# The per-token rows of an mLSTM head, copied to all partitions by DMA inside SBUF instead of by products, and the next head's weights moved right behind the scores

## The reference

```
m_t = max(max_s d, b + m_old)          d = b_t - b_s + i_s   (s <= t)
w   = exp(d - m_t)                      s = (q k) * w
num = sum_s s v + inter part            den = sum_s s + inter part
h   = num / max(|den|, exp(-m_t))       then RMSNorm of h over the head's 256 channels
```

## Time and profile before

| what | value |
|---|---|
| median of 3 runs | 1712.9 us (1712.69 to 1718.42) |
| the profiled execution: time, span | 1710.33 us, 1708.5 us |
| PE busy, of the span | 1655.7 us, 97% |
| DVE, ACT busy | 765.4 us, 554.6 us |
| stage `states`, roughly | 553 to 618 us of the span |
| stage `heads`, roughly | 618 to 699 us |

### The profile page before, as it was taken

The page is one execution under the profiler, slowest core; times in us unless marked ns, Lnnn a source line. Parts: engine busy times, 40 slices in busy tenths (PEclk is TensorE's granted clock), DMA queues, the critical chain, the costliest instruction groups (busy, mean ns, idle before and its releaser), DMA issues.

```text
span 1708.5 us, 30634 instructions
## 1 busy us (share of the span) xinstructions
PE 1655.7 (97%) x12836; PEld 1568.2 (92%) x12836; DVE 765.4 (45%) x1150; ACT 554.6 (32%) x845; POOL 4.2 (0%) x20
## 2 busy tenths in 40 slices
PE   7999999999999889999999999989999999999996
PEld 7999999999988667999999977679999999999996
DVE  4333333333682443553337678664453333333332
ACT  5222222222333432542111257562233222222222
POOL 0000000000000000000000000000000000000000
PEclk9999999999999999999999999999999999999998
DMA  5222223222322740233333240643322222223221
GB/s 139 77 86 86 86 86 98 88 85 76 77 75 56 242 153 1 74 87 86 100 92 98 72 183 26 203 145 97 86 87 87 86 86 86 86 86 102 86 85 53
DMA packets 253836, 161.77 MB, mean 95 GB/s; under 512 B 8234, under 2 KB 246047, under 8 KB 253762
## 3 DMA queue, kind: packets, MB, share of 16 engines
q1 hardware_dynamic: 253616, 160.67, 32.3%
q10 hardware_dynamic: 146, 0.04, 0.0%
HBM read 143.14 MB, written 16.40 MB: 93 GB/s over the span
## 4 chain that ended last, share of the span: by engine, by line
PE 88%; ACT 3%; DVE 3%; DMA 3%; issue 1%; SPq 1%; ACTq 0%; DVEq 0%
PE ps L402 73%; PE ps L781 2%; PE ps L969 2%; PE ps L933 1%; PE ps L1257 1%; PE ps L1185 1%; PE ps L1128 1%; PE ps L1301 1%; PE ps L1018 1%; DMA Cb<-in_state_C 1%; DVE small L2329 1%; PE ps L1113 1%; PE ps L1182 1%; PE ps L1260 1%; DMA raw<-in_w_in 0%
## 5 line engine op out<-in xcount | busy, mean ns | idle before, releaser
L402 PE MATMUL ps<-xn_hi,w_hi 128*128 128x272 f32 (+1 forms) x2192 | 635.7, 290 | 5.6 <-DVE w_lo L374 3.4
L402 PE MATMUL ps<-xn_hi,w_lo 128*128 128x272 f32 (+1 forms) x2192 | 637.5, 291 | 0.0
L402 PE MATMUL ps<-xn_lo,w_hi 128*128 128x272 f32 (+1 forms) x2192 | 634.5, 289 | 0.0
L370 ACT ACTIVATE w_hi<-raw 128x1024 fp32r<-128x1024 f32 (+1 forms) x200 | 222.2, 1111 | 823.4 <-PE ps L402 819.6
L402 PEld LDWEIGHTS ps<-xn_hi,w_hi 128*128 128x128 f32 x2192 | 413.6, 189 | 7.2 <-DVE w_lo L374 4.0
L402 PEld LDWEIGHTS ps<-xn_hi,w_lo 128*128 128x128 f32 x2192 | 413.5, 189 | 0.0
L402 PEld LDWEIGHTS ps<-xn_lo,w_hi 128*128 128x128 f32 x2192 | 412.5, 188 | 0.0
L374 DVE TENSOR_TENSOR w_lo<-raw,w_hi 128x1024 fp32r<-128x1024 f32 (+1 forms) x200 | 257.6, 1288 | 214.0 <-ACT w_hi L370 213.6
L402 PE MATMUL ps<-h_lo,w_hi 128*128 128x280 f32 (+1 forms) x704 | 204.7, 291 | 0.0
L402 PE MATMUL ps<-h_hi,w_hi 128*128 128x280 f32 (+1 forms) x704 | 204.7, 291 | 0.0
L402 PE MATMUL ps<-h_hi,w_lo 128*128 128x280 f32 (+1 forms) x704 | 204.6, 291 | 0.0
(11 more groups left out here) (372 smaller groups left out, 2026.8 us busy)
## 6 DMA issues: line engine op xcount, KB each, us to landing
raw<-in_w_in SPq DMA_DIRECT2D x56, 512.0 KB, 3.8
raw<-in_ffn_w_gate SPq DMA_DIRECT2D x44, 512.0 KB, 3.8
raw<-in_ffn_w_up SPq DMA_DIRECT2D x44, 512.0 KB, 3.8
raw<-in_ffn_w_down SPq DMA_DIRECT2D x32, 704.0 KB, 4.5
Cb<-in_state_C SPq DMA_DIRECT2D x32, 256.0 KB, 4.1
out<-Cb SPq DMA_DIRECT2D x32, 256.0 KB, 3.0
pages<-in_cache_k SPq DMA_DIRECT2D x16, 512.0 KB, 4.7
pages<-in_cache_v SPq DMA_DIRECT2D x16, 512.0 KB, 4.9
```

What stands on the lines that cost most here:

```text
L370: act.activation(w_hi[s][:, 0:p.nk, :], raw[s][:, 0:p.nk, :], ACT.Copy).then_inc(hi_done[s], 1)
L402: mm = pe.matmul(ps[:, bank + half, 0:p.half], w[s][:, k, :], x[:, k0 + k, cols], start=first and k == 0 and a == 0, stop=last and k == p. ...
```

## The change

The `spread` products are gone, and with them the copies on ACT. In their place SP issues eight transfers inside SBUF: one row of `rows` on one partition is the source, read 128 times (a dimension of step 0), and all 128 partitions of a buffer are written. Four go for row 2 (`load_max`, head 0 into `tM`, the others into `rowb`), four for row 3 (`load_m`, into `rowb[:, 2]`). ACT reads that buffer in its exp and moves the exp behind `weights(h+1)`. DVE moves `weight_arg(h+1)` ahead of `mean_square(h-1)`. From head 2 on `scores(h)` waits for `u_ready`, since banks 0 and 1 hold the sums of `squares_sum` until then.

```diff
+        rowb = at("rowb", [128, 3, T], f32, R + 2 * D * 4 + 5568)
+        def max_row(h):
+            return rowb[:, h % 2, :] if h else tM[:, :]
...
+            def every_partition(row, h):
+                return rows[h:h + 1, row, :].unsqueeze(1).to_broadcast([1, 128, T])
+            def load_max(h):
+                if h >= 3:
+                    sp.wait_ge(wt_ready, h - 1)
+                sp.dma_start(max_row(h), every_partition(2, h)).then_inc(bM_full[h % 2], 16)
+            def load_m(h):
+                if h >= 1:
+                    sp.wait_ge(bm_ready, h)
+                sp.dma_start(rowb[:, 2, :], every_partition(3, h)).then_inc(bm_full, 16)
+            load_max(0)
...
             begin(sp, "heads")
-            stream(p_om)
+            load_max(1)
+            load_max(2)
+            load_m(0)
+            for s in range(2):
+                load(sp, p_om, 0, s)
+            load_m(1)
+            load_max(3)
+            load_m(2)
+            load_m(3)
+            stream(p_om, 1)
...
-            spread(0, 2).then_inc(bM_full, 1)
...
-                pe.wait_ge(bM_ready, h + 1)
+                if h >= 2:
+                    pe.wait_ge(u_ready, h - 1)
                 score(ps[:, 0, 0:SPLIT], 0, 0, SPLIT)
...
-                    if blk == 2:
-                        if h >= 1:
-                            pe.wait_ge(u_ready, h)
-                        else:
-                            pe.wait_ge(p_ready, 6)
-                        spread(h, 3).then_inc(bm_full, 1)
-                    if blk == 3 and h + 1 < HM:
-                        pe.wait_ge(bm_ready, h + 1)
-                        spread(h + 1, 2).then_inc(bM_full, 1)
...
             for h in range(HM):
-                act.wait_ge(bm_full, h + 1)
-                act.activation(tok(rstd[:, :]), two(0), ACT.Exp, bias=con[:, C_LNE:C_LNE + 1], scale=2.0).then_inc(bm_ready, 1)
                 if h + 1 < HM:
-                    act.wait_ge(bM_full, h + 2)
-                    copy(tok(tA[:, :]), two(0)).then_inc(bM_ready, 1)
                     weights(h + 1)
-                else:
+                act.wait_ge(bm_full, 16 * (h + 1))
+                if h >= 1:
+                    act.wait_ge(u_ready, h)
+                act.activation(rstd[:, :], rowb[:, 2, :], ACT.Exp, bias=con[:, C_LNE:C_LNE + 1], scale=2.0).then_inc(bm_ready, 1)
+                if h + 1 == HM:
                     split_hi(act, p_om, 0, 0)
...
+                if h + 1 < HM:
+                    weight_arg(h + 1)
                 if h >= 1:
                     mean_square(h - 1, 0)
                 if h + 1 < HM:
-                    weight_arg(h + 1)
                     masks(h + 1)
```

More of the change, by code:

```diff
@@ L223, in build @@
         assert R + 6 * D * 4 + 8192 + T * 4 <= RQ
+        rowb = at("rowb", [128, 3, T], f32, R + 2 * D * 4 + 5568)
+        assert 2 * D * 4 + 5568 + 3 * T * 4 <= 6 * D * 4
+        def max_row(h):
+            return rowb[:, h % 2, :] if h else tM[:, :]
         ofac = at("ofac", [128, HD, T], f32, RV)
@@ L540, in build @@
         fill_full, fill_done = sem("fill_full"), sem("fill_done")
-        bM_full, bM_ready, bm_full, bm_ready = sem("bM_full"), sem("bM_ready"), sem("bm_full"), sem("bm_ready")
+        bM_full, bm_full, bm_ready = [sem(f"bM_full{i}") for i in range(2)], sem("bm_full"), sem("bm_ready")
         wt_ready, we_ready, om_gated = sem("wt_ready"), sem("we_ready"), sem("om_gated")
@@ L1194, in _ @@
                 values(h)
-            pe.wait_ge(bm_ready, HM)
+            pe.wait_ge(u_ready, HM - 1)
             pe.wait_ge(evac[0], p_om.ev0)
@@ L1673, in _ @@
                         copy(npo, ps[:, 7, 0:DHM]).then_inc(fill_done, 1)
-            act.wait_ge(bM_full, 1)
-            copy(tok(tM[:, :]), two(0)).then_inc(bM_ready, 1)
             c_out(7)
@@ L2153, in weight_arg @@
             def weight_arg(h):
-                v.wait_ge(bM_ready, h + 1)
-                P, m = P6[h % 2], tA if h else tM
+                v.wait_ge(bM_full[h % 2], 16 * (h // 2 + 1))
+                P, m = P6[h % 2], max_row(h)
                 for blk, (t0, nt) in enumerate(HBLOCKS):
```

## The result

The changed kernel takes **1734.2 us** (median of 5 runs, 1730.1 to 1735.9) against 1716.0 us of the kernel before on the same chip (5 runs, 1712.7 to 1718.4). The ratio is **1.0105, 95% interval 1.0088 to 1.0122**: slower by 18 us, between 15 and 21. The forecast was 15.6 us slower.

The account below looks back on a forecast made before the run. PE, busy 97%, bounds the kernel; the 13.2 us removed leave the path to queued transfers. Heads begin 5.6 us later and the second `om` product ends the sum at +15.6: 1712.9 + 15.6 = 1728.5 us, range 1708 to 1740.

Parts of the forecast that it names:

- The price of one transfer: Each of eight broadcasts inside SBUF: all 128 packets share one path, 10.2 us at 28 GB/s; chance 0.70.
- the 80 ns of a packet alone: Earlier `qkv` to `xrot` transfers: a 2240-byte packet with the path to itself takes 80 ns.
- The 200 and 330 ns of packets together: Same `qkv` to `xrot` transfer: 11 packets average 200 ns, the first three 330 ns each, so neighbouring partitions share a path.
- Rival 1: Transfers run side by side, 0.64 to about 3 us each, no deadline missed: 1699.7 us; chance 0.15.
- The heads: From head 0 on, exps of row 3 wait for queued transfers; second `om` product at 714.3 instead of 698.71.
- The clock: Slower PE clock after idling in heads: costed at nothing, products wait for transfers anyway; uncovered, up to 1.7 us per stretch.
- PE's idle time: Sign in the profile after: PE idle over 15 us before `values(1)`.
- The `states`: Head 0's maxima transfer delays state loads 6.4 us; less 0.8 for the removed spread, heads begin 5.6 us later.
- 3.8 us said to be free: In `states`, DMA slack between the first four stores landed (562.8) and the load issued at 566.6.
- What is removed: Eight spreads of 1.23 us and stalls of 1.28 us: 0.8 in `states`, 11.2 in heads 0-2, 1.2 in head 3; 13.2 us.
- The slope and break-even: Whole kernel: each microsecond per transfer costs 8 us from 9.5 us up, 4 below; break-even at about 7.5 us.
- rival 2: Transfers partly shared, 5 to 9 us each: -10 us at 5, -2 at 7, +6 at 9; 1703 to 1719; chance 0.08.

Follow-up runs that it names:

- e_order: The change with m of head 0 issued ahead of the maxima of head 2 instead of behind them; 1.0108 of the kernel before, +18.5 us.
- e_twice: The change with a ninth, unused transfer of the same kind ahead of m of head 0; 1.0177 of the kernel before, +30.3 us.
- e_near: The change with each head's rows first copied to four neighbouring partitions, each read 32 times; 1.0110 of the kernel before, +18.8 us.
- e_own: The change with every partition reading its own row (128 sources, wrong numbers, only time counts); 0.9905 of the kernel before, -16.3 us.
- e_far: The change with each head's rows first copied to four partitions 28 apart, each read 32 times; 0.9916 of the kernel before, -14.4 us.
- e_first: The change with head 0's maxima by the old product and ACT copy, the seven other transfers kept; 1.0066 of the kernel before, +11.3 us.
- e_32: The change with each head's rows on four partitions 32 apart, each read 32 times; 0.9975 of the kernel before, -4.3 us.
- e_pair: The change with each head's rows on two partitions 64 apart, each read 64 times; 0.9982 of the kernel before, -3.1 us.

## Why the prediction was right, step by step

**The price of one transfer** (taken at the high bound, 10.2 us at 28 GB/s): 10.6 at 27 GB/s. The reading of the earlier trace rows, that packets of neighbouring partitions share a path, is shown by the pair of neighbouring and distant copies. What carries the price is the 80 ns of a packet alone: 10.6 us are 83 ns for each of the 128. The 200 and 330 ns of packets together are upper bounds, since they put the whole 2.2 us down to 11 packets, and the same rows hold 16 more under 512 bytes. Rival 1 (side by side) fell; it is what the kernel does once the source is spread. Of the two rules of the Trainium skill, page "SBUF — State Buffer", that the prediction weighed, the section "Door 1: The DMA port swizzle" (27.6 GB/s for partitions 0 to 3) is the one that the trace agrees with, 27; the 436 GB/s of its summary come near only with 128 sources, 364.

**The heads**, from SP's begin of the heads:

| | predicted | measured |
|---|---|---|
| m of head 0 landed | 32.0 | 33.3 |
| m of head 1 | 45.4 | 46.7 |
| m of head 2 | 65.9 | 67.8 |
| m of head 3 | 78.2 | 80.5 |
| second `om` product | 87.9 | 90.3 |
| against before | +10.0 | +12.4 |

The order and the waits are those foreseen; the 2.4 us too few come with the transfer's 10.2 us for 10.6 to 10.7 (seven of them in a row would make 3). The clock was costed at nothing here, and from 650 us on, while PE came to stand, it was 0.68, 0.66 and 0.50 in three stretches of 5 us; as said, the products behind it were waiting for transfers anyway. ACT waits for a DMA before all four exps; the prediction named three and took head 1's (5.79 us) as hidden. DVE's waits of 7.85 and 2.08 us before `weight_arg` (line 2173) of heads 1 and 3 it did not name. PE's idle time is 14.61 us where it said over 15, and stands not before `values(1)` but before the fifth score piece ahead of it; from 668 to 671 us, where the remaining scores run, the granted clock is 0.50, the 1.2 GHz level.

**The `states`** (6.4 of delay, less 0.8: +5.6): +8.4. The mechanism is the one foreseen, and a term is missing from it. The changed kernel's stage and its waits for state loads:

```profile
556.99:632.61 75.62, 63.46 (x534) 45.77 (x534) 30.66 (x64) 27.73 (x53) 0.00 (x0) 0.91 0.76 214
```

```profile
PE ps L814 <- DMA Cb<-in_state_C: 9.7, 3, 4.9
```

Set against the kernel with 128 sources, which runs the same 534 products: waits for state loads 9.7 against 5.3 us, +4.4; PE busy 63.46 against 58.27 us at a mean clock of 0.91 against 1.00, **+5.2 for the same products**. 4.4 + 5.2 = 9.6 = 75.62 - 66.06.

The delay was about rightly sized. The load behind the stores is issued 17.9 us after the stage's first load, for 13.0 before: 5.0 us later for the 6.4 foreseen. In e_order, e_twice and e_near, where a transfer of 10.6 us stands at the same place, it is 6.0, 5.7 and 7.3 us later, and PE waits 6.9, 7.5 and 4.7 us more for state loads than in e_own. The clock is the term that was wrong: costed at nothing and expected only in the heads, it made more than half of the loss here, and in those three kernels PE's busy time for the same products is 6.1, 7.5 and 4.0 us longer. A wait of the change and the group of products behind it, the granted clock there, and the same group in e_own:

```profile
584.21 1.11 PE L814 MATMUL ps<-con,Cb 128*128 128x128 f32 x4 [4.86 <-DMA Cb<-in_state_C]
...
590.19 0.38 PE L814 MATMUL ps<-con,tA 128*128 128x128 f32 x2
```

```profile
580.00:585.00 5.00, 0.79 (x4) 0.80 (x5) 0.99 (x3) 0.00 (x0) 0.00 (x0) 0.65 0.89 256
585.00:590.00 5.00, 5.00 (x24) 4.25 (x23) 0.00 (x0) 2.27 (x4) 0.00 (x0) 0.66 0.93 293
```

```profile
584.13 0.66 PE L814 MATMUL ps<-con,Cb 128*128 128x128 f32 x4 [0.85 <-DMA Cb<-in_state_C]
...
588.11 0.38 PE L814 MATMUL ps<-con,tA 128*128 128x128 f32 x2
```

The group takes 5.98 us in the one and 3.98 us in the other: PE stood for 4.86 us and then ran part of the time at 1.2 GHz. These sizes are not steady: the four kernels lost 8.1 to 13.4 us in `states` against the kernel before, at mean clocks of 0.93 to 0.87.

The clock can also cost where PE waits no longer in all. The transfer of e_far takes 2.9 us, less than the 3.8 us said to be free, and its waits for `Cb` are 5.1 us, as before; yet it lost 4.4 us, for PE's busy time is 63.2 us, 5.0 more than in e_own. Its waits are fewer and longer: 0.72, 2.40 and 1.96 us, where e_own has four from 0.85 to 1.68 us and the full clock throughout. The length of a wait doesn't decide alone. Four products behind a wait in e_far, and the same four in e_first, whose `states` have no such transfer:

```profile
596.25 1.11 PE L819 MATMUL ps<-con,Cb 128*128 128x128 f32 x4 [2.40 <-DMA Cb<-in_state_C]
```

```profile
593.37 0.66 PE L812 MATMUL ps<-con,Cb 128*128 128x128 f32 x4 [2.62 <-DMA Cb<-in_state_C]
```

Behind 2.40 us of standing they take 1.11 us, behind 2.62 us 0.66 us. What decides between the two stays open.

**What is removed** (13.2 us): with quick transfers the heads take 63.9 us, in four kernels to a tenth, against 77.9: 14.0 us where the prediction's 11.2 + 1.2 had 12.4. The stalls of 1.28 us are gone as said. A spread costs more than its 1.23 us, which were read from the gap in front of its successor. The four products behind it also take longer: 1.02 us until the next row of before (from 650.34),

```profile
651.36 0.62 PE L1185 MATMUL ps<-P,ones 128*128 128x272 f32 x2
```

and 0.91 in the kernel with 128 sources:

```profile
659.13 1.08 PE L1202 MATMUL ps<-P,vtok 128*128 128x272 f32 x4
660.04 0.62 PE L1202 MATMUL ps<-P,ones 128*128 128x272 f32 x2
```

That makes 1.34 each, and the two of head 0 give 2.67 (from the third score piece to the last product of `values`, 13.85 and 11.18 us); 7 x 1.34 and 3 x 1.28 are 13.2 of the 14.0, the last 0.8 us are not placed. In `states` the removed spread gave 1.2 us (e_own), for the 0.8 taken. The 13.2 are thus small by some 2 us; in the changed kernel that is under the wait for the transfers.

**The slope and break-even** (8 us for one above 9.5, 4 below, even at 7.5 us): e_32 and e_pair put the transfer at 5.3 us, where the list of rival 2 gives -9 us. The prediction's own terms, 13.2 us removed and 4 us for each microsecond over 3.8 to 3.9, give -7.4 there and break-even at 7.1; the list and the 7.5 don't follow from them. Measured -4.3 (-6.5 to -1.9) and -3.1 (-5.0 to -1.2). In the heads alone they win 5.7 and 5.9 us, and the working has 12.4 - 3 x 1.4 = 8.2. In e_32 the transfer that comes late is m of head 0, used 19.4 us after the begin of the heads; behind it:

```profile
647.67 1.81 PE L1158 MATMUL ps<-qm,km 128*128 128x144 f32 x8 [5.35 <-DVE P L2198]
```

5.35 us of wait, and then products at a clock of 0.50 (the window of 648 to 650 above): 8.3 us lost against 63.9 for a wait of 5.35. Here PE is the bound again right behind the stall, so the cover for the clock that the prediction named is gone, and its price of "up to 1.7 us" was too small: 8.3 - 5.35 = 3 us. Break-even is near 6.3 us a transfer, not 7.5: an estimate by a straight line from -4 us at 5.3 to +18 at 10.6, with no run between.

The sum, 15.6 for 18.2, thus held by a transfer sized within 4% and by the order and the waits that were foreseen. That it came within 2.6 us is in part luck: in the profile the two stages lost 20.8 us (8.4 and 12.4), and PE's slower clock in `states`, 5.2 us, stood in no term.

## What to carry to other kernels

Cost a transfer inside SBUF by how many ports its *source* reaches, even where its destination is all 128 partitions, as here: a broadcast from one partition ran at 27 GB/s with all 16 engines on it, and the cure is a source elsewhere: a small copy in device memory, or a few copies at distances that reach other ports (four copies 28 apart turned +18 into -14 us, four neighbours did nothing). In a stage that alternates between stores and loads, and wherever PE is the bound again behind a wait, cost a new wait at its length plus the slow clock behind it, which made such waits here cost half as much again (5.35 us, 8.3 lost) to twice as much (4.4 and 9.6). Look at how the waits are cut up and not only at their sum: e_far waited no longer for its loads than the kernel with 128 sources and lost 5.0 us to the clock. And the longest wait in a view is not the one worth removing if the same queue is full behind it.

## What was not expected of the hardware

- Sixteen engines show 87 to 90% busy at 27 GB/s: a high DMA share says nothing of bytes moved.
- SP itself is held up: with three such transfers under way the issue of two weight panels took 20.82 us (1.35 us in the kernel with 128 sources), so issues on SP are not free behind a slow transfer.
- A transfer whose source is `[4, 32, T]` kept a quarter of the engines' time busy, one of `[2, 64, T]` an eighth, and one of `[1, 128, T]` nearly all of it: how a pattern is written sets how many engines work on it. From one port four engines gave 28 GB/s and all sixteen 27, so more engines didn't help there. The Trainium skill, page "DMA: Bandwidth & Descriptors", section "Rules for kernel authors", says that an outermost dimension of c copies below 16 confines a transfer to at most c engines; the shares of the engines here (0.24 and 0.26 for 4, 0.13 for 2) agree.
